# Query up-projection weights by transfers of their own, and key-side mean squares between the halves of the low-rank query product

## The reference, cut to what matters

```
hk = modulate(rms_norm(x, kv_norm_g), k_shift, k_scale)
kv_a = hk @ w_kv_a                        # 1024 -> 256 + 32
c_kv, k_rope = split(kv_a, [256])
c_kv = rms_norm(c_kv, kv_a_norm_g)
kv = (c_kv @ w_kv_b)                      # -> 16 heads x (64 key + 64 value)
k_nope = rms_norm(k_nope); k_rope = apply_rope(rms_norm(k_rope))
h = modulate(rms_norm(x, norm1_g), shift1, scale1)
q = rms_norm(h @ w_dq, q_norm_g) @ w_uq   # 1024 -> 256 -> 16 heads x (64 + 32)
q_nope = rms_norm(q_nope); q_rope = apply_rope(rms_norm(q_rope))
```

## Time and profile before

| | us |
|---|---|
| median of 3 runs | 1273.59 (1272.74 to 1275.84) |
| the profiled execution's own time | 1275.22 |
| its span in the profile | 1273.4 |
| TensorE busy | 1237.6 (97%) |
| VectorE busy | 860.0 (68%) |
| ScalarE busy | 604.7 (47%) |
| DMA, mean rate | 194 GB/s |

### The profile page before, as it was taken

The page is one execution under the profiler, slowest core; times in us unless marked ns, Lnnn a source line. Parts: engine busy times, 40 slices in busy tenths (PEclk is TensorE's granted clock), DMA queues, the critical chain, the costliest instruction groups (busy, mean ns, idle before and its releaser), DMA issues.

```text
span 1273.4 us, 25334 instructions
## 1 busy us (share of the span) xinstructions
PE 1237.6 (97%) x10911; PEld 1159.2 (91%) x10911; DVE 860.0 (68%) x1221; ACT 604.7 (47%) x790; POOL 48.2 (4%) x65
## 2 busy tenths in 40 slices
PE   6989999999999999999999999999999999999997
PEld 5768999999865599999999999999999999999997
DVE  6897899987448776668566655448369666666443
ACT  6844743433535754444455344336335546544342
POOL 4300001000000000000000000000000000000000
PEclk9999999999999999999999999999999999999998
DMA  9896589877455558554565554564554334655452
GB/s 269 262 307 225 188 291 311 295 263 238 155 205 176 188 178 285 169 194 128 189 213 174 182 171 137 181 186 127 162 167 135 138 128 154 208 170 194 151 173 74
DMA packets 219544, 246.49 MB, mean 194 GB/s; under 512 B 5840, under 2 KB 209056, under 8 KB 219456
## 3 DMA queue, kind: packets, MB, share of 16 engines
q1 hardware_dynamic: 211616, 218.63, 52.9%
q0 software_dynamic: 7488, 26.34, 6.1%
q10 hardware_dynamic: 352, 0.23, 0.1%
HBM read 244.14 MB, written 1.05 MB: 193 GB/s over the span
## 4 chain that ended last, share of the span: by engine, by line
PE 84%; DVE 5%; DMA 5%; ACT 4%; issue 2%; ACTq 0%; SPq 0%; DVEq 0%
PE PS L1768 82%; ACT PARTS L605 1%; DVE WL L1054 1%; DMA RING<-in_ada_w 1%; DVE ARENA L1076 1%; DMA RING<-in_ffn_w_gate 1%; DMA RING<-in_s_w_glu 1%; DMA RING<-in_ffn_w_down 1%; ACT ARENA L724 1%; DVE ARENA L1172 1%; DMA RING<-in_mla_w_uq 0%; DVE X L1176 0%; DMA ACC<-in_c 0%; PE PS L2103 0%; DVE PARTS L1032 0%
## 5 line engine op out<-in xcount | busy, mean ns | idle before, releaser
L1768 PE MATMUL PS<-PARTS 128*128 128x256 f32 (+3 forms) x3608 | 840.4, 283 | 0.0
L1768 PEld LDWEIGHTS PS<-PARTS 128*128 128x128 f32 (+1 forms) x3608 | 619.5, 189 | 1.4 <-issue 0.9
L1054 DVE TENSOR_TENSOR WL<-RING,PARTS 128x2048 fp32r<-128x2048 f32 (+2 forms) x189 | 387.2, 2052 | 216.6 <-ACT PARTS L605 216.1
L1768 PE MATMUL PS<-HH,WL 128*128 128x258 f32 (+3 forms) x1832 | 521.1, 284 | 2.3 <-DVE PARTS L1032 1.3
L1768 PE MATMUL PS<-HH,PARTS 128*128 128x258 f32 (+3 forms) x1832 | 519.0, 283 | 0.0
L605 ACT CAST PARTS<-RING 128x2048 fp32r<-128x2048 f32 (+2 forms) x189 | 324.1, 1717 | 284.9 <-DMA RING<-in_w_ffn_out 69.3
L1768 PEld LDWEIGHTS PS<-HH,WL 128*128 128x128 f32 (+1 forms) x1832 | 345.3, 188 | 7.0 <-issue 5.8
L1768 PEld LDWEIGHTS PS<-HH,PARTS 128*128 128x128 f32 (+1 forms) x1832 | 345.0, 188 | 0.4
L1768 PE MATMUL PS<-PARTS,WL 128*128 128x256 f32 (+1 forms) x832 | 236.8, 285 | 1.6 <-DVE WL L1054 0.8
L1768 PEld LDWEIGHTS PS<-PARTS,WL 128*128 128x128 f32 x832 | 158.2, 190 | 3.6 <-issue 2.5
L1768 PE MATMUL PS<-ARENA 128*32 128x63 f32 (+9 forms) x864 | 59.8, 274 | 4.9 <-issue 3.8
(11 more groups left out here) (346 smaller groups left out, 962.7 us busy)
## 6 DMA issues: line engine op xcount, KB each, us to landing
RING<-in_w_ffn_in SPq DMA_DIRECT2D x44, 1024.0 KB, 5.1
RING<-in_ada_w SPq DMA_DIRECT2D x32, 1024.0 KB, 8.0
RING<-in_ffn_w_gate SPq DMA_DIRECT2D x22, 1024.0 KB, 5.3
RING<-in_ffn_w_up SPq DMA_DIRECT2D x22, 1024.0 KB, 5.2
RING<-in_w_in SPq DMA_DIRECT2D x20, 1024.0 KB, 5.2
ARENA<-in_ada_w POOLq DMA_DIRECT2D x16, 1024.0 KB, 7.5
RING<-in_ffn_w_down SPq DMA_DIRECT2D x16, 768.0 KB, 4.6
RING<-in_w_ffn_out SPq DMA_DIRECT2D x16, 768.0 KB, 4.4
```

What stands on the lines that cost most here:

```text
L1054: V.tensor_tensor(WL[:, u % SLOTS, 0:w], RING[:, u % SLOTS, 0:w], WH[:, u % SLOTS, 0:w].bitcast(fp32), SUB)\
L1768: return nc.tensor.matmul(o, lhsT, rhs, start=start, stop=stop)
```

## The change

The two ring units `uq` go. Instead GpSimd issues four DMAs straight from `w_uq` in memory into `WQN` and `WQR`, with the head's columns picked by the transfer. The two for `WQN` (one for each 128 rows of the weight; runs of 64 floats) stand in GpSimd's loop ahead of the loads of half-slabs 10 and 12, and wait for the first pair of FFN 0. The two for `WQR` (runs of 32 floats) stand behind the load of half-slab 19 and wait for the last pair of FFN 0. `WQR` moves to `S5_AT`. VectorE's four `packed` copies of `uq` go; TensorE waits for `uq_loaded`.

The key side's mean squares are issued between the two blocks of `dq`, ScalarE makes their reciprocal roots there, and only the query side's mean square is left behind `dq`. `ada_cols` of both slabs and `rot` move from ahead of `project(0)` to behind `project(1)`, VectorE's work on `KR` and its `modulation(64, 72)` move with them, and `keep_warm(2, 5)` goes. The diff, with renamed counters left out:

```diff
-        WQR, at = arena(at, 2, HEADS1 * ROPE)
+        WQR, _ = arena(S5_AT, 2, HEADS1 * ROPE)
...
-        stream("uq", w_view("mla_w_uq", 0), (0, 2), 0, 1536, 768)
...
+            UQ = A["mla_w_uq"][0].rearrange("(k p) (h c) -> p k h c", p=P, c=QK1)
             for n in range(2 * len(ADA_FFN0 + ADA_FFN1)):
+                if n in (10, 12):
+                    k = (n - 10) // 2
+                    pool.wait_ge(S["unit_done"], AT["ffn0"] + 2)
+                    pool.dma_start(WQN[:, k, :].rearrange("p (h c) -> p h c", c=NOPE), UQ[:, k, :, 0:NOPE]).then_inc(S["uq_loaded"], 16)
                 if n == 2 * len(ADA_FFN0):
+                    pool.wait_ge(S["unit_done"], AT["ffn0"] + 2 * MT)
+                    for k in range(2):
+                        pool.dma_start(WQR[:, k, :].rearrange("p (h c) -> p h c", c=ROPE), UQ[:, k, :, NOPE:]).then_inc(S["uq_loaded"], 16)
                     pool.wait_ge(S["unit_done"], AT["wo"] + 4)
...  (ScalarE)
+            act.wait_ge(S["kv_stat"], 1)
+            nc.scalar.activation(STD[:, 0:SEQ], PS[:, 5, 0:SEQ], ACT.Ln, bias=eps)
+            link(nc.scalar.activation(SDH[0:ROPE, 0, 0:SEQ], PS[0:ROPE, 6, 0:SEQ], ACT.Ln, bias=eps[0:ROPE]))
+            nc.scalar.activation(STD[:, 0:SEQ], STD[:, 0:SEQ], ACT.Exp, scale=-0.5).then_inc(S["kv_std"], 1)
+            nc.scalar.activation(SDH[0:ROPE, 0, 0:SEQ], SDH[0:ROPE, 0, 0:SEQ], ACT.Exp, scale=-0.5).then_inc(S["kv_std"], 1)
             act.wait_ge(S["unit_done"], AT["dq"] + 1)
             for b in range(3, 5):
                 nc.scalar.activation(SQ[:, b, 0:SEQ], PS[:, b, 0:SEQ], ACT.Square).then_inc(S["kv_sq"], 1)
-            act.wait_ge(S["kv_stat"], 1)
-            nc.scalar.activation(STD[:, :], PS[:, 5, :], ACT.Ln, bias=eps)
-            ...
+            act.wait_ge(S["kv_stat"], 2)
+            link(nc.scalar.activation(STD[:, SEQ:], PS[:, 5, SEQ:], ACT.Ln, bias=eps))
+            nc.scalar.activation(STD[:, SEQ:], STD[:, SEQ:], ACT.Exp, scale=-0.5).then_inc(S["kv_std"], 1)
...  (VectorE)
-            for c in range(2):
-                packed("uq", c, QK1, NOPE, ROPE, WQR, "uq_packed")
...
-            for c in range(2):
-                packed("uq", c, QK1, 0, NOPE, WQN, "uq_packed")
...  (TensorE)
+            for b in range(2):
+                for k in range(KT):
+                    if b == 0:
+                        pe.wait_ge(S["h_ready"], KT * 2 + k + 1)
+                    ins = mm(PS[:, 3 + b, 0:SEQ], w[:, k, b * P:(b + 1) * P], H[:, k, 0:SEQ], k == 0, k == KT - 1)
+                if b == 1:
+                    ins.then_inc(S["unit_done"], 1)
+                    pe.wait_ge(S["kv_std"], 2)
+                    pe.wait_ge(S["kv_sq"], 5)
+                else:
+                    pe.wait_ge(S["kv_sq"], 3)
+                    mm(PS[0:ROPE, 6, 0:SEQ], blk32[0:ROPE, 0:ROPE], SQ[0:ROPE, 2, 0:SEQ], True, True)
                 for k in range(2):
+                    ins = mm(PS[:, 5, b * SEQ:(b + 1) * SEQ], ones256, SQ[:, 3 * b + k, 0:SEQ], k == 0, k == 1)
+                ins.then_inc(S["kv_stat"], 1)
             ada_rows(ADA_LAST)
             ada_rows(ADA_LAST + 1)
             pe.wait_ge(S["kv_norm"], 1)
-            ada_cols(ADA_LAST)
-            ada_cols(ADA_LAST + 1)
-            mm(PS[0:ROPE, 7, 0:SEQ], rot[0:ROPE, 0:ROPE], KR[0:ROPE, 0, :], True, True).then_inc(S["kr_rot"], 1)
-
-            keep_warm(2, 5)
...
                 if s < 6:
-                    pe.wait_ge(S["uq_packed"], s + 2 if s < 2 else 3 + i // 2)
+                    pe.wait_ge(S["uq_loaded"], 64)
...
             for s in range(10):
                 project(s)
+                if s == 1:
+                    ada_cols(ADA_LAST)
+                    ada_cols(ADA_LAST + 1)
+                    mm(PS[0:ROPE, 7, 0:SEQ], rot[0:ROPE, 0:ROPE], KR[0:ROPE, 0, :], True, True).then_inc(S["kr_rot"], 1)
                 if s >= 1:
                     mean_square(s - 1)
```

More of the change, by code:

```diff
@@ L423, in x_of @@
             return X[:, :, TALL - N_TOK[n]:TALL]
-        HP_LAST = {1: 1, 5: 2}
-        HP_COUNT = {s: s + 1 - sum(t < s for t in HP_LAST) for s in range(10)}
         HP_GAIN = ["mla_q_rope_norm_g"] * 2 + ["mla_q_nope_norm_g"] * 4 + ["k_nope_norm_g"] * 4
@@ L1444, in _ @@
                 V.scalar_tensor_tensor(CKV[:, i, :], PS[:, i, 0:SEQ], vec("kv_a_norm_g", i), STD[:, 0:SEQ], MUL, MUL)
-                V.scalar_tensor_tensor(QA[:, i, :], PS[:, 3 + i, 0:SEQ], vec("mla_q_norm_g", i), STD[:, SEQ:], MUL, MUL)
             V.scalar_tensor_tensor(KR[K, 0, :], PS[K, 2, 0:SEQ], VEC[K, VAT["k_rope_norm_g"]:VAT["k_rope_norm_g"] + 1],
-                                   SDH[K, 0, 0:SEQ], MUL, MUL).then_inc(S["kv_norm"], 1)
+                                   SDH[K, 0, 0:SEQ], MUL, MUL)
+            dve.wait_ge(S["kv_std"], 3)
+            for i in range(2):
+                ins = V.scalar_tensor_tensor(QA[:, i, :], PS[:, 3 + i, 0:SEQ], vec("mla_q_norm_g", i), STD[:, SEQ:], MUL, MUL)
+            ins.then_inc(S["kv_norm"], 1)
             def packed(label, c, width, c0, n, dst, done):
@@ L1457, in _ @@
             V.tensor_scalar(GQ[:, 1:2], vec("mla_q_nope_norm_g", 0), SCALE1, None, MUL)
-            for c in range(2):
-                packed("uq", c, QK1, NOPE, ROPE, WQR, "uq_packed")
[L1460 to L1467, removed]
-            for c in range(2):
-                packed("uq", c, QK1, 0, NOPE, WQN, "uq_packed")
             def raw(s):
[L1474 to L1477, removed]
+                dve.wait_ge(S["hp_proj"], s + 1)
                 V.tensor_copy(RAW[s], PS[:, s % 2, :]).then_inc(S["hp_raw"], 1)
@@ L1514, in _ @@
                 raw(s)
+                if s == 1:
+                    dve.wait_ge(S["rope_sin"], 1)
+                    dve.wait_ge(S["kr_rot"], 1)
+                    V.tensor_tensor(KR[K, 1, :], PS[K, 7, 0:SEQ], SINQ[K, :], MUL)
+                    link(V.tensor_tensor(KR[K, 2, :], KR[K, 0, :], COSQ[K, :], MUL))
+                    V.tensor_tensor(KR[K, 1, :], KR[K, 1, :], KR[K, 2, :], ADD).then_inc(S["dve_step"], 1)
+                    steps[0] += 1
+                    dve.wait_ge(S["ada_cols"], ADA_LAST + 2)
+                    modulation(64, 72, PS[:, 6, 384:392])
                 if s == 2:
@@ L2216, in _ @@
             ins.then_inc(S["unit_done"], 1)
-            linear(AT["dq"], [3, 4], H, SEQ, first=("h_ready", KT * 2))
-            pe.wait_ge(S["kv_sq"], 5)
-            for i, (b, c0) in enumerate(((0, 0), (3, SEQ))):
+            u = AT["dq"]
+            loaded(u)
+            w = slot(u, KT, 256)
+            for b in range(2):
[10 more added lines that the diff above has]
+                    mm(PS[0:ROPE, 6, 0:SEQ], blk32[0:ROPE, 0:ROPE], SQ[0:ROPE, 2, 0:SEQ], True, True)
                 for k in range(2):
-                    mm(PS[:, 5, c0:c0 + SEQ], ones256, SQ[:, b + k, 0:SEQ], k == 0, k == 1)
-            mm(PS[0:ROPE, 6, 0:SEQ], blk32[0:ROPE, 0:ROPE], SQ[0:ROPE, 2, 0:SEQ], True, True).then_inc(S["kv_stat"], 1)
+                    ins = mm(PS[:, 5, b * SEQ:(b + 1) * SEQ], ones256, SQ[:, 3 * b + k, 0:SEQ], k == 0, k == 1)
+                ins.then_inc(S["kv_stat"], 1)
             ada_rows(ADA_LAST)
@@ L2244, in project @@
                         ins = mm(PS[:, s % 2, j * SEQ:(j + 1) * SEQ], w[:, k, c0:c0 + P], src[:, k, :], k == 0, k == 1)
-                ins.then_inc(S["unit_done"] if s in HP_LAST else S["hp_proj"], 1)
+                ins.then_inc(S["hp_proj"], 1)
             def mean_square(s):
```

5 lines of the change are left out of this document (1 added, 4 removed).

## The result

| | before | after |
|---|---|---|
| median, 20 runs each | 1275.15 us (1271.97 to 1277.52) | 1278.47 us (1273.72 to 1285.20) |
| the profiled execution's own time | 1275.22 | 1276.39 |
| its span | 1273.4 | 1274.6 |
| from the first matmul of FFN 0 to the first of `kva` | 202.39 | 204.76 |
| from the first `ada_rows` to `mean_square(0)` | 13.31 | 10.48 |

The ratio after to before is 1.0032, 95% interval 1.0018 to 1.0045: slower by 0.3%, about 4.1 us. The forecast was 1.6 us faster. A second and a third profile of the same kernel, among the experiments, show more.

A forecast was written before the change was run, and what follows sets the result against it. TensorE, busy 97% of the span, was taken as the bound, with `uq`'s load setting the start of `project(0)`. MLA -2.93, `WQN` +1.0 and `WQR` +0.3 gave -1.6 us, a median of 1272.0 us; range 1269.3 to 1276.3.

The forecast's parts named there:

- Mean squares in two parts: In MLA around `dq`: splitting the squares gains TensorE 0, could be 0.3 us worse if the extra drain shows.
- `ada_gap`'s last unit: Issued 1.48 us later, behind `dq`, landing at 361.5 before TensorE needs it: cost 0, at most 0.4 us.
- `ada_rows` to `mean_square(0)`: In MLA: gain 2.93 us, 1.64 from the unused matmuls with the wait, 1.29 from projections at full clock.
- the clock falls anyway: Rival, 20%: thin work in MLA still brings 1.2 GHz over full work, costing 1.7 us; total +0.1, 1273.7 us.
- `WQN`'s first transfer: In FFN 0: delays the gate unit's landing, through VectorE to TensorE's wait at 259.8; +1.0 us.
- `WQN`'s second transfer: In FFN 0 at 223.3: meets a unit VectorE takes only at 237.4; costs 0 to 1 us.
- `WQR`, +0.3: End of FFN 0: two transfers behind half-slab 19 make a down unit 1.6 us late against slack 1.3; +0.3 us.
- FFN 0 pays more than MLA gets: Rival, 12%: short runs go ahead of ring loads, VectorE falls back, TensorE waits for sums at 259.8; +2.6, 1276.2 us.

The follow-up runs named there:

- e6_cols_first: `e1_late` with `ada_cols` of both slabs and `rot` back ahead of `project(0)`, without the unused matmuls; 1275.4 us, ratio to before 1.0003.
- e2b_rope_late: Second set of the changed kernel with only the two `WQR` transfers moved behind FFN 0, `WQN` staying; 1279.29 us, ratio to before 1.0019.
- e9_nope_twice: The changed kernel with `WQR` behind FFN 0 and each `WQN` transfer issued twice in FFN 0; 1280.41 us, ratio to before 1.0044.
- e1_late: The changed kernel with all four transfers issued behind FFN 0, at 331 us; 1273.67 us, ratio to before 0.9985.
- e5_nope_late: The changed kernel with only the two `WQN` transfers moved behind FFN 0, `WQR` staying; 1274.65 us, ratio to before 0.9999.
- e4_transfers_alone: The kernel before with only the four transfers added in FFN 0, their data unused, MLA's order as before; 1278.77 us, ratio to before 1.0033.
- a0_after_again: The changed kernel itself run and profiled a second time, nothing altered; 1276.27 us, ratio to before 1.001.
- a1_after_once_more: The changed kernel itself run and profiled a third time, nothing altered; 1279.58 us, ratio to before 1.0028.
- e2_rope_late: First set of the changed kernel with only the two `WQR` transfers moved behind FFN 0, `WQN` staying; 1278.17 us, ratio to before 1.0025.

## Why the prediction was wrong

The step that failed is the price of the transfers in FFN 0: +1.0 for `WQN` and +0.3 for `WQR`, 1.3 us together, where the stage got longer by 2.4, 6.1 and 4.6 us in the three profiles of the change. The way from a late ring load over VectorE to TensorE was right. How late the loads come, and what a stall costs behind its end, was not. Point by point, by its own steps:

- *Mean squares in two parts, 0, up to +0.3.* Right: +0.26. "Could be 0.3 worse if the extra drain shows" is what came.
- *`ada_gap`'s last unit, 0.* Right: no wait in the second `ada_rows`.
- *`ada_rows` to `mean_square(0)`, -2.93.* Right in size, -2.83, and in the order. The 1.64 for the unused matmuls with the wait is safe, since that work is gone. For the 1.29 of the clock no run shows the reason: `e6_cols_first` has the gain with `ada_cols` ahead, in one profile, and in the old order the clock fell in both profiles. The rival "the clock falls anyway" did not happen in the three profiles of the change, but it did in `e2b_rope_late` and `e9_nope_twice`, one projection later, for 1.5 us. Its "7.6 us of thin work" is 6.9 with the wait for the copy, by the earlier trace rows (358.10 to 365.02).
- *`WQN`'s first transfer, +1.0.* The wait at 260 was 1.3, 2.2 and 1.9 us in the three profiles of the change, 0.2 before; but `e1_late` has 1.2 there without the transfer. The term was of the right size for the quick execution and too small for the others. The medians say so more strongly: with `WQN` alone in FFN 0 the ratios are 1.0025 and 1.0019, with everything late 0.9985, which is 4 to 5 us for `WQN`.
- *`WQN`'s second transfer, "costs 0 to 1".* In the sum it had 0. It failed in part: the loads of 224 and 230 landed after 11.2 and 8.3 us instead of 7.4 and 5.1 in the first profile of after, which VectorE's slack still took. In `e2b_rope_late` the late loads ended in the stall at 238 to 241.
- *`WQR`, +0.3: **the term that the profiles of the change exceed most**.* I let the transfers queue behind half-slab 19 and make the down unit late by 1.6 us, against a slack of 1.3. The unit was late by 2.5 in the first profile and 3.7 in the second, and the stall was 1.1, 3.2 and in the third 2.1, in `e5_nope_late` 2.5, in `e4_transfers_alone` 4.3 (there a unit earlier). Before, low parts cost 0.8. Standing behind a load on the same queue did not keep them from the ring loads. I took the price of the transfers' engine time and set it against one landing alone; the following units were late by 2.7 and 2.5 in the first profile as well (5.8 to 8.5 us, 4.4 to 6.9), and beside `WQR` half-slab 19 was still in flight (issued at 289.29, 8.7 us). The Trainium skill (DMA: Bandwidth & Descriptors, Queues, rings and completion order) says that each DMA engine takes turns between the queue rows that have work, a packet at a time. The later landings agree with that, 7.7 to 10.2 and 11.4 us; no run here shows the turns themselves.
- *What was left out: a stall costs more than its length.* Around the end of the stalls of 3.2, 4.3 and 5.7 us, and behind one of 1.9 and one of 2.4, the clock fell to 1.2 GHz for a while, 1.4 to 1.6 us more in the two further profiles of the change (202.67 and 202.82 us busy against 201.24). Behind five others of 2.0 to 2.5 us it did not fall (2.2 in `a0_after_again`, 2.1 in `a1_after_once_more`, 2.0 in `e4_transfers_alone`, 2.2 in `e2b_rope_late`, 2.5 in `e5_nope_late`), so the length alone does not decide. The sum had a low clock for MLA alone.

The rival "FFN 0 pays more than MLA gets" is what happened, at 12%. Its price for the stage, 5.7 less 0.2 with everything going wrong, is of the size that the profiles have: longer by 2.4, 6.1 and 4.6, against a gain of 2.57 in MLA. It decides from a loss of 2.93 on, and two of three profiles are past that. But its mechanism named only the sums at 259.8; some half of the added waiting is for low parts of down units (1.0, 2.4 and 1.3 us, against 1.1, 2.0 and 1.7 for the sums at 260). I held the small wait of 0.2 us against it. That a wait is small says nothing about the slack behind it: VectorE was busy 14.68 of 15 us and the DMA engines 0.92, and those rows were the better witness.

The medians differ by 3.3 us (4.1 by the ratio); with MLA's 2.57 that makes 5.9 to 6.7 lost, where the three profiles' mean for FFN 0 is 4.4. The rest is not accounted for. The size of the loss is itself uncertain: the three sets of runs gave 1.0032, 1.001 and 1.0028. Part may be a fall of the clock at 953 us, far behind the change, worth 1.5 us (the same work takes 15.09 us from 952.40 on in after and 13.58 from 952.79 on in before): after had it in two of its three profiles, before not in its one; over all fourteen profiles it is in seven, with the transfers late or not. Why one execution of the same kernel loses 6 us in FFN 0 and another 2.4 stays open too. The spread of `e2_rope_late`, 1268 to 1284, against that of `e5_nope_late`, 1274 to 1277, may point at `WQN`, but `e6_cols_first`, with nothing new in FFN 0, runs from 1272 to 1283 as well.

## What to carry to other kernels

A transfer moved out of a stage that waits for it is not free because it is early: it is paid in the stage that now holds it, and there the rows to read are the busy shares of the DMA engines and of the engine fed by them, not the waits of the engine at the end, which stay small until the slack is used up and then jump. Put it where both have room: the same four transfers cost some 4 us at 210 to 300 and nothing that shows at 331. There the change came out 0.15% faster, with an interval that just excludes no change; three kernels built on it gave 0.9985, 0.999 and 1.0003. When a change bundles several edits, price each alone: here one (no packing wait, no unused matmuls) made the gain as far as the profiles show, two gave nothing in one profile each, and one made the loss.

## What the runs showed of the hardware that was not expected

- Two GpSimd transfers of 0.25 MB in runs of 128 bytes, issued a few us ahead of or beside a ring load of 0.75 MB, moved its landing from 7.7 to 10.2 and 11.4 us; with long runs it was 9.0. Over all profiles it was 7.0 to 8.0 without them and 10.2 to 11.4 with them.
- Some stalls of TensorE of 1.9 to 5.7 us between dense products brought a stretch at 1.2 GHz. It began 1.5 us after the work had come back from the 1.9 us stall of `a1_after_once_more` (back at 261.40, 0.96 at 262 to 263, 0.50 at 263 to 264), and just before it did in `a0_after_again` (3.2 us; 0.95 at 306 to 307, work back at 307.08); in the longest, 5.7 us, the granted clock was already 0.68 at 242 to 244, before the work came back at 244.24. Other stalls of 2.0 to 2.5 us brought none.
- The same thin work at the beginning of MLA (32-wide products, one-column products, `rot`) brought the low clock with the unused matmuls behind it, in both profiles that had them, and in two of twelve without them (`e2b_rope_late`, `e9_nope_twice`).
- Issuing one of the transfers took GpSimd 1.17 us (256-byte runs, 0.5 MB) and 1.15 us (128-byte runs, 0.25 MB), against 0.75 for a load of 1 MB in long runs.
